# Down weights in 8 KB packets, and gate and up weights read at every second column, in a 16-expert streaming layer on one core

## What is computed

```python
D_MODEL, D_EXPERT, N_EXPERTS, TOP_K = 1024, 256, 16, 2
for e in range(N_EXPERTS):
    he = jax.nn.silu(h2 @ w_gate[e]) * (h2 @ w_up[e])
    moe = moe + combine[..., e:e + 1] * (he @ w_down[e]).astype(jnp.float32)
x = x + moe.astype(x.dtype)
```

## Time and profile before

| | us |
|---|---|
| median of three runs | 429.23 |
| the profiled execution | 429.25 |
| its span, first to last instruction | 427.5 |
| PE busy | 410.3 |
| DVE, ACT, POOL busy | 274.8, 197.8, 125.2 |
| the stretch 245 to 420 us, the experts | 175.0 |

### The profile page before, as it was taken

How to read it: one execution, slowest core, us unless ns; L and a number is a source line. 1 busy time by engine, 2 the same in 40 slices (tenths; PEclk the granted TensorE clock), 3 DMA queues, 4 the chain that set the end, 5 groups by cost and what they waited for, 6 DMA issues and landing times.

```text
span 427.5 us, 7800 instructions
## 1 busy us (share of the span) xinstructions
PE 410.3 (96%) x2924; PEld 358.8 (84%) x2925; DVE 274.8 (64%) x663; ACT 197.8 (46%) x486; POOL 125.2 (29%) x210
## 2 busy tenths in 40 slices
PE   7899999999999999999999999999999999999992
PEld 3687999998777776777886799999999999999991
DVE  3856430805759898636447898745557777776894
ACT  5566230704666666333112734444445555555723
POOL 2012000200044234351000323333335555554343
PEclk9999999999999999999999999999999999999997
DMA  8971703506000029943214789999999989989321
GB/s 276 286 203 51 234 2 104 204 2 203 4 1 3 0 85 420 371 181 148 100 69 151 255 298 422 332 410 379 351 353 344 382 307 337 349 313 366 112 88 50
DMA packets 32074, 91.37 MB, mean 214 GB/s; under 512 B 11200, under 2 KB 11712, under 8 KB 27942
## 3 DMA queue, kind: packets, MB, share of 16 engines
q1 hardware_dynamic: 20790, 71.97, 45.6%
q0 software_dynamic: 11248, 18.93, 12.5%
HBM read 86.38 MB, written 26.01 MB: 263 GB/s over the span
## 4 chain that ended last, share of the span: by engine, by line
PE 84%; DVE 6%; ACT 4%; issue 3%; DMA 1%; POOL 0%; SPq 0%; DVEq 0%; ACTq 0%; POOLq 0%
PE ps L1225 25%; PE ps L835 10%; PE ps L837 9%; PE ps L836 9%; PE ps L1265 4%; PE ps L1266 3%; PE ps L1270 3%; PE ps L1218 3%; PE ps L999 2%; PE ps L964 2%; PE ps L1233 2%; DMA region_x<-in_x_prompt 1%; PE ps L982 1%; PE ps L1035 1%; PE ps L831 1%
## 5 line engine op out<-in xcount | busy, mean ns | idle before, releaser
L1225 PEld LDWEIGHTS ps<-region_p,region_a 128*128 128x128 f32 x512 | 58.3, 192 | 1.0 <-DVE region_p L2106 0.4
L1225 PE MATMUL ps<-region_p,region_a 128*128 128x128 f32 x512 | 58.5, 275 | 0.0
L837 PE MATMUL ps<-region_a_r,region_w_r 128*128 128x288 f32 x192 | 56.5, 294 | 0.0
L835 PE MATMUL ps<-region_a_r,ring_r 128*128 128x288 f32 x128 | 40.5, 317 | 0.0
L836 PE MATMUL ps<-region_a_r,ring_r 128*128 128x288 f32 x128 | 37.7, 295 | 0.0
L837 PEld LDWEIGHTS ps<-region_a_r,region_w_r 128*128 128x128 f32 x192 | 36.0, 188 | 0.0
L1640 ACT ACTIVATE region_p<-ps,gffn_sb 128x128 f32<-128x128 f32 x116 | 31.6, 385 | 7.3 <-PE ps L1218 7.1
L1661 ACT ACTIVATE region_t<-ps 128x256 f32<-128x256 f32 x15 | 5.8, 383 | 56.6 <-PE ps L1225 56.6
L708 POOL DMA_INDIRECT region_x<-h_rows,lists x13 | 16.6, 1281 | 45.7 <-DVE slot_w L2209 33.7
L835 PEld LDWEIGHTS ps<-region_a_r,ring_r 128*128 128x128 f32 x128 | 24.0, 188 | 6.8 <-issue 3.3
L1225 PEld LDWEIGHTS ps<-region_p,ring 128*128 128x128 f32 x256 | 29.1, 192 | 0.8 <-DVE region_p L2128 0.5
(11 more groups left out here) (381 smaller groups left out, 1027.7 us busy)
## 6 DMA issues: line engine op xcount, KB each, us to landing
region_a<-in_w_gate SPq DMA_DIRECT2D x8, 1024.0 KB, 10.3
region_a<-in_w_up SPq DMA_DIRECT2D x8, 1024.0 KB, 15.6
region_a<-in_w_down SPq DMA_DIRECT2D x8, 1024.0 KB, 18.5
region_w<-in_w_in SPq DMA_DIRECT2D x2, 2048.0 KB, 11.0
region_w<-in_w_out SPq DMA_DIRECT2D x2, 2048.0 KB, 8.1
ring<-in_w_gate SPq DMA_DIRECT2D x4, 1024.0 KB, 8.7
ring<-in_w_up SPq DMA_DIRECT2D x4, 1024.0 KB, 17.9
ring<-in_w_down SPq DMA_DIRECT2D x4, 1024.0 KB, 10.1
```

The costliest lines, as they stand in the source:

```text
L835: pe.matmul(out, lhs_hi, rhs_hi, start=first, stop=False)
L837: return pe.matmul(out, lhs_lo, rhs_hi, start=False, stop=last)
L1225: ins = pe.matmul(ps[:, 2 + b, (first + c) * P:(first + c + 1) * P], w[:, k, c * P:(c + 1) * P], xT[:, b, k, :], start=(k == 0), stop=(k = ...
```

## The change

The view of the down weights takes rows 2p and 2p+1 for partition p, 8 KB in a row. Chunk c of the features then holds the features 2p+c, and gate and up take columns c, c+2, c+4 and so on as stationary operand instead of columns 128c to 128c+127. Shapes, tiles, the order of all instructions, semaphores and the number of transfers stay.

```diff
-        wd_v = w_down.rearrange("a e (c p) n -> (a e) p c n", p=P)
+        wd_v = w_down.rearrange("a e (p c) n -> (a e) p c n", p=P)
...
-                            ins = pe.matmul(ps[:, 2 + b, (first + c) * P:(first + c + 1) * P], w[:, k, c * P:(c + 1) * P],
+                            ins = pe.matmul(ps[:, 2 + b, (first + c) * P:(first + c + 1) * P], w[:, k, c:FE:FC],
                                             xT[:, b, k, :], start=(k == 0), stop=(k == KC - 1))
...
-                            ins = pe.matmul(ps[:, LAST_BANKS[c], at:at + P], w[:, k, c * P:(c + 1) * P],
+                            ins = pe.matmul(ps[:, LAST_BANKS[c], at:at + P], w[:, k, c:FE:FC],
                                             xT[:, b, k, :], start=(k == 0), stop=(k == KC - 1))
```

## The result

The changed kernel takes 435.47 us (435.27 to 435.67, 4 runs) against 430.12 (428.21 to 433.93, 4 runs). The ratio on record is 1.0111, 95% interval 1.0072 to 1.0150; the two medians divided give 1.0124, within that interval. By the threshold of 2% that is no change, by the interval it is slower. The profiled executions, taken alike, are 427.5 and 433.9 us long; their difference, 6.4 us, is what has to be found.

The account below looks back on a forecast made before the run. PE was taken to bound the expert stage, busy 174.07 of 175.00 us. Down loads 0 plus stationary operands 0, all else unchanged, gave 429.2 us from the profiled 429.25; range 427.0 to 438.6.

Parts of the forecast that it names:

- part 1: Down loads of the experts: 4 KB runs become 8 KB; gain between 0 and 0.93 us, taken as 0.
- part 2: Gate and up's stationary columns 8 bytes apart, 1024 loads: cost between 0 and 47.5 us, taken as 0.
- a part of the penalty: Rival in gate and up: plain loads grow by part of 50 ns, say half, 21.9 us more: 451; chance 0.05.
- the price of the step between columns: Gate and up's stationary loads: between 0 and 50 ns each for the step, taken as 0.
- the cover: Gate and up: load occupancy 108 ns against spacing 111.6, so 4 ns free before growth costs time.
- 82 ns of latency: Plain float32 load of 128 columns lasts 190 ns: 108 occupancy, the other 82 latency that overlaps.
- 192 ns or at most a few more: Sign of a right forecast: duration of line 1225's loads, with gate and up still 7.14 us an expert.
- the upper bound: Gate and up's stationary loads: a step costs at most 50 ns each, from transposes' loads; 47.5 us in all.
- the strict reading: Stationary loads: each additional 16-byte line costs; 32 more lines cost 17 ns, load 125 ns, sum 13.7 us more: 443.
- the lenient one: Stationary loads: two accesses in a 16-byte line hide the penalty, which 8 bytes just keep; sum 429.2.
- late gathers: Rival: gathers sharing DMA engines with down loads land 6.5 us later, PE stops 9.4 us: 438.6; chance 0.03.

Follow-up runs that it names:

- the wide runs: Kernel before with gate and up's moving operand doubled to 256 columns, all experts but the last, stationary steps 1, 2, 3: 528.84, 529.95, 535.02 us.
- the wide run with step 3: Kernel before with 256 moving columns in gate and up for all experts but the last, stationary columns 3 floats apart: 535.02 us.

## Why the prediction was wrong

**Right.** The change sits in gate and up and the down loads alone, PE bounds the stage, the packet counts are those forecast to the packet, and part 1 is worth 0: 1.0021 with an interval that holds 1. No gather came so late that PE waited; no wait for one stands in the chain.

**Wrong: part 2, the stationary operand at 0.** Measured 6.1 ns for each of 1024 loads, 6.2 us. What came is the case that was given as a part of the penalty, at 0.05, though with far less than the half that was reckoned there. The step of the working that failed is the price of the step between columns; the cover was mis-sized too, by less.

*The price.* "Separate columns can be fetched at 0.84 ns each however far they lie apart" rested on one coincidence: the transposes' load with 32 bytes between columns lasts 190 ns, and so does a plain load of neighbours; no row had a plain load with a step. The run with 8 floats has just this distance in a plain load, and it is 335 ns long, spaced 236. The step doesn't bring the load to a common pace. It takes the plain load from 0.87 to 1.85 ns a column (spacing over 128 columns), and the transposes' load, by the prediction's own estimate of 82 ns of latency, from (141 - 82) / 128 = 0.46 to (190 - 82) / 128 = 0.84. That eight transposes took 0.88 us with the step and 0.87 without was then no sign of a free step: by the same estimate the load with the step takes 108 ns, which fits into the 109 ns that a transpose takes anyway, cover of the sort that the wide runs show. No run shortened the transposes' matmul, so for them this is argued, not shown.

*The cover.* "108 ns for 128 ... 4 ns are free" took the load's occupancy from how durations grow with columns. The run with 64 moving columns puts it at 110.8 ns of the 111.6, so 0.8 ns were free and not 3.6. That alone would have left the forecast where it was, since no growth was charged. The busy time of PEld could not have settled it. PEld is busy for 7.14 of 7.14 us here, but the loads of line 1218 have no idle time ahead of them either, where a load 50 ns longer did not change the pace, and in the wide run with step 3, where the matmul sets the pace, PEld has 110.8 us busy and 0.7 idle. A load lasts longer than the spacing in all three, 192, 141 and 251 ns, so one is always under way.

One sign that the prediction gave for being right misleads for the same reason: a load of "192 ns or at most a few more". It came to 196, and gate and up took 7.53 us all the same.

So the upper bound was wrong as well. 50 ns, from the transposes, was taken as the most that a step can cost; in plain loads it costs up to 124.8. It did no harm only because 8 bytes lie below the cliff, which was luck. By the rule of the Trainium skill that the prediction drew on (SBUF — State Buffer, section Door 1), the strict reading gave 443, the lenient one 429.2; measured was 435.5. Going from 32 lines to 64 cost 6.1 ns where the strict reading had 17, and two hits on a line weren't quite free.

The time lies in the range, 427.0 to 438.6, but by luck: the upper part of the range was put there for late gathers, and none stopped PE.

## What to carry to other kernels

A PEld that is busy for the whole of a stretch may or may not set the pace, since loads overlap; halving the moving operand tells, and where the spacing stays, every ns that the load grows is paid. A step between stationary columns of float32 added 5% to the spacing at 8 bytes and about doubled it from 16 bytes on, and cost nothing at 8 and 12 bytes beneath a matmul of 256 columns; so a layout that makes a DMA nicer should put its step on an operand whose load is covered. And the longer packets were worth nothing here, where no transfer was waited for.

## What the runs showed that was not expected

A plain float32 product with 128 moving columns is bound by its load and not by the moving columns, if only just: 64 moving columns take 110.8 ns a record, 128 take 111.6, 256 take 215.8. Half of the last, 107.9 ns, is an estimate of what the matmul alone would take with 128. With 16 floats between columns the load is quicker (216.7 ns) than with 4 or 8 (231.4, 236.4); no run tells why. Nor does one tell where the 6.1 ns at a step of 2 come from.
